# Grid attention tiled by 16 grid columns and 8 rows, in place of two whole grid rows

## The chip, the cores and the metric

The kernel runs on one core of a Trainium2 chip. The metric is the device time of one execution, in microseconds: the median of three was 2283.3 before the change (2283.01 to 2284.41). All times below are microseconds unless marked ns.

## What is computed

Two blocks run one after the other on 512 tokens of width 1024, in float32. The first has two layers of mixed attention and a gated product. The second has two layers: window and latent attention over the tokens and 256 context tokens, and then the grid attention, which is what changes. The 512 tokens are a grid of 8 rows and 64 columns. A query at column c sees, in all 8 rows, the 16 columns from clip(c - 8, 0, 48), with a learned bias by the distance in rows and columns, and beside them all 256 context keys, in one softmax:

```python
rows = s_len // GRID_W                      # 8, GRID_W = 64
kh = min(C_KH, rows)                        # 8
cs = jnp.clip(col - C_KW // 2, 0, GRID_W - C_KW)
col_ok = (col[None, :] >= cs[:, None]) & (col[None, :] < cs[:, None] + C_KW)
...
s_loc = jnp.einsum('bqhd,bkhd->bhqk', qr, kr) * scale + bias
s_loc = jnp.where(mask, s_loc, -jnp.inf)    # mask: col_ok for each of the 8 rows
s_ctx = jnp.einsum('bqhd,blhd->bhql', qr, kc) * scale
p = jax.nn.softmax(jnp.concatenate([s_loc, s_ctx], axis=-1), axis=-1)
return p_loc @ vr + p_ctx @ vc              # 16 heads of 64
...
y = (o * jax.nn.silu(z)) @ out_w
```

## The kernel before, in words

Every engine runs its own program, a list of stages, and stages pass work on by semaphores. Products (line 526) split each factor into a high and a low float32r part and add three matmuls; TensorE takes weights in pieces from two buffers, which ScalarE (`cut_high`, L486) and VectorE (`cut_low`, L491) cut ahead of it.

`WidePairs` (L1712) is the attention of the second block, with `grid=True` for the grid. It walks 8 units, one for each pair of heads, and in each 4 steps, one for each tile of 128 queries, which are two grid rows. Keys of a step are all 512 tokens and 256 context tokens, 768 for each head. Both heads of a step lie in three banks of PSUM, in one of two sets (`base`, L1800), so that TensorE computes the scores of step s+1 before it transposes step s. For each step:
- TensorE, `scores` (L1840): three terms for each head, keys of 512 and 256 columns, in the order `ORDER`. `turn_probs` (L1886): 12 transposes of 128x128. `values` (L1898): 24 matmuls, 6 key tiles for 2 heads, into bank 6. Once a unit `wide` (L1913): 4 transposes of the inverse sums into bank 7.
- VectorE, `grid_iteration` (L2149): `context_max` (L2070), the copy of the first transposed bank (L2116), then for each head an add of the bias with a running maximum (L2086) and its negation (L2088). Once a unit `invert` (L2104, L2109), `pair_low` for the queries and the keys of the next unit (L2211), and `gate_wide` (L2143), inverse sums by silu(z).
- ScalarE: the exponentials (L1971), the copy of the other two transposed banks (L1982), and once a unit `pair_high` (L2206), `copy_o` (L1989), which empties bank 6, and the loads of z and of the bias (L2004, L2007).
- GpSimd: the product of the outputs and the gate (L2193).

The order on ScalarE, in which a step's instructions stand behind each other, is:

```python
for s in range(-1, self.N + 1):
    if 0 <= s < self.N and self.rest[s]:
        copy_probs(s)
    if s + 1 < self.N:
        exps(s + 1)
    ...
    if s - 1 in self.ends:
        copy_o(self.ends[s - 1])
```

The bias: `Start.gpsimd` writes the table of 15x31 values of each head, padded, to a scratch in HBM. `MaskedBias` (L2231), beside the down product of the first layer (`WideProduct.scalar`, L1522), loads shifted windows of it (4 DMAs for a pair of heads, L2247, issued by ScalarE between its cuts), GpSimd adds the column mask (L2259), and the result is stored (L2251). Queries, and the outputs in `Split`, are reversed within a grid row (`backwards`), since the bias is read backwards. `ModNorm` (L2800) is the norm ahead of the second layer: for each of 8 chunks VectorE makes `full` (L2899) and `low` (L2906) with ScalarE's `h_hi` between (L2861), and the product that follows starts while these run. `SiluOut` (L1204) and `CopyOut` (L1113) empty the banks of the products for z and for the queries.

## Time and profile before

| | before |
|---|---|
| median of 3 runs | 2283.3 |
| span of the profiled execution | 2281.6 |
| TensorE busy | 2230.1 (98%) |
| VectorE busy | 1283.6 (56%) |
| ScalarE busy | 925.7 (41%) |
| GpSimd busy | 280.3 (12%) |
| granted TensorE clock, mean | 0.999 |

The span goes from the first to the last instruction of one profiled execution. Its own time is given only as this span; the runs of the table's first row contain in addition what lies around it, 1.7 between the span and the median. A busy share is an average over all stages; the chain of waits says which engine the end waits for. L numbers are lines of the kernel. PE is TensorE, DVE VectorE, ACT ScalarE, POOL GpSimd, PEld the loading of weights, and a name with q the queue of an engine.

### The profile page before, as it was taken

Reading aid. Unit: us, or ns where it says so; the run is one execution under the profiler, and the core shown is the slowest. Engines: PE = TensorE matmul, PEld = TensorE weight load, DVE = VectorE, ACT = ScalarE, POOL = GpSimd, SP = SyncE. Lnnn points to the kernel's source line nnn. Section 1 sums busy time; section 2 is a strip of 40 time slices with the busy share of each in tenths; the row PEclk is TensorE's granted clock in tenths of the full one; section 3 lists DMA queues with packets and bytes.
Section 4 is the critical chain, followed back from the end, with each engine's and each line's share of the span. In section 5 each row is a group of like instructions: output and inputs, shape, how many; then the busy total and the mean of one; then the engine's idle time right before and its main releaser. Section 6 shows DMA issues by size and latency. Waiting matters only on the chain.

```text
span 2281.6 us, 33000 instructions
## 1 busy us (share of the span) xinstructions
PE 2230.1 (98%) x13479; PEld 1852.9 (81%) x13479; DVE 1283.6 (56%) x1884; ACT 925.7 (41%) x1558; POOL 280.3 (12%) x175
## 2 busy tenths in 40 slices
PE   7999999999999999999999999999999999999998
PEld 7876688888888776788888888888888888888887
DVE  4687548964225778459853235414667462225884
ACT  3447743222214347742222223224655342124773
POOL 2001322121332002222111000000100000000000
PEclk9999999999999999999999999999999999999999
DMA  5220025632893210035532421221000214212221
GB/s 161 88 70 2 1 94 181 202 114 75 209 266 89 77 56 1 20 129 185 166 111 75 143 88 48 83 79 42 19 18 16 78 62 164 74 56 75 69 66 56
DMA packets 149417, 205.80 MB, mean 90 GB/s; under 512 B 42485, under 2 KB 95746, under 8 KB 149250
## 3 DMA queue, kind: packets, MB, share of 16 engines
q1 hardware_dynamic: 110288, 169.83, 22.9%
q10 hardware_dynamic: 38914, 33.69, 5.7%
q8 instruction: 107, 1.75, 0.3%
q14 instruction: 44, 0.36, 0.0%
q0 software_dynamic: 64, 0.16, 0.0%
HBM read 188.85 MB, written 14.82 MB: 89 GB/s over the span
## 4 chain that ended last, share of the span: by engine, by line
PE 91%; DVE 4%; ACT 3%; issue 2%; DMA 0%; ACTq 0%; POOLq 0%; DVEq 0%
PE ps L526 68%; PE ps L1858 4%; PE ps L1892 3%; PE ps L2509 3%; PE ps L1909 2%; PE ps L2526 2%; PE ps L2538 2%; DVE probs_t L2116 1%; PE ps L2514 1%; PE ps L733 1%; ACT probs_t L2615 1%; DVE neg_max L2060 1%; PE ps L533 1%; PE ps L2512 1%; PE ps L2546 1%
## 5 line engine op out<-in xcount | busy, mean ns | idle before, releaser
L491 DVE TENSOR_TENSOR w_low<-w_raw,w_high 128x2048 fp32r<-128x2048 f32 (+4 forms) x140 | 303.5, 2168 | 491.6 <-ACT w_high L486 491.4
L486 ACT ACTIVATE w_high<-w_raw 128x2048 fp32r<-128x2048 f32 (+4 forms) x140 | 253.0, 1807 | 602.0 <-PE ps L526 549.9
L526 PE MATMUL ps<-h_hi,w_high 128*128 128x512 f32 (+1 forms) x1168 | 439.6, 376 | 1.2 <-DVE w_low L491 0.6
L526 PE MATMUL ps<-h_lo,w_high 128*128 128x512 f32 (+1 forms) x1168 | 437.3, 374 | 0.0
L526 PE MATMUL ps<-h_hi,w_low 128*128 128x512 f32 (+1 forms) x1168 | 436.9, 374 | 0.0
L526 PEld LDWEIGHTS ps<-h_hi,w_high 128*128 128x128 f32 x1168 | 220.0, 188 | 42.1 <-DVE w_low L491 1.2
L526 PEld LDWEIGHTS ps<-h_hi,w_low 128*128 128x128 f32 x1168 | 219.8, 188 | 39.6
L526 PEld LDWEIGHTS ps<-h_lo,w_high 128*128 128x128 f32 x1168 | 220.0, 188 | 39.3 <-issue 0.5
L526 PE MATMUL ps<-w_high,h_hi 128*128 128x512 f32 (+3 forms) x576 | 214.0, 372 | 0.6 <-DVE h_lo L2906 0.6
L526 PE MATMUL ps<-w_low,h_hi 128*128 128x512 f32 (+3 forms) x576 | 211.6, 367 | 0.0
L526 PE MATMUL ps<-w_high,h_lo 128*128 128x512 f32 (+3 forms) x576 | 211.4, 367 | 0.0
L720 DVE SCALAR_TENSOR_TENSOR ada_acc<-ada_w,cond,ada_acc 128x512 f32<-128x512 f32 x168 | 143.6, 896 | 2.6
L1473 POOL TENSOR_TENSOR gated<-gated,inv_wide 128x512 f32<-128x512 f32 x44 | 96.6, 2215 | 370.4 <-ACT gated L1465 370.4
L526 PE MATMUL ps<-act_hi,w_low 128*128 128x512 f32 x352 | 137.0, 389 | 0.0
L526 PE MATMUL ps<-act_lo,w_high 128*128 128x512 f32 x352 | 137.0, 389 | 0.0
L526 PE MATMUL ps<-act_hi,w_high 128*128 128x512 f32 x352 | 136.9, 389 | 0.0
L1971 ACT ACTIVATE probs<-ps,neg_max 128x768 f32<-128x768 f32 (+3 forms) x160 | 123.4, 783 | 13.8 <-DVE neg_max L2060 9.7
L526 PEld LDWEIGHTS ps<-w_high,h_hi 128*128 128x128 f32 x576 | 108.2, 188 | 22.4 <-issue 7.5
L526 PEld LDWEIGHTS ps<-w_low,h_hi 128*128 128x128 f32 x576 | 108.2, 188 | 16.0
L526 PEld LDWEIGHTS ps<-w_high,h_lo 128*128 128x128 f32 x576 | 108.3, 188 | 15.1
L1468 ACT ACTIVATE act_hi<-gated 128x512 fp32r<-128x512 f32 x44 | 27.6, 633 | 197.1 <-DVE gated L1486 196.4
L2670 DVE TENSOR_REDUCE neg_max<-ps 128x2 f32<-128x256 f32 (+1 forms) x80 | 65.7, 822 | 64.0 <-PE ps L2512 35.4
(372 smaller groups left out, 3869.8 us busy)
## 6 DMA issues: line engine op xcount, KB each, us to landing
w_raw<-in_w_gate_up SPq DMA_DIRECT2D x44, 1024.0 KB, 5.2
ada_w<-in_ada_w SPq DMA_DIRECT2D x24, 1024.0 KB, 5.2
w_raw<-in_w_down SPq DMA_DIRECT2D x20, 1024.0 KB, 5.3
w_raw<-in_w_in SPq DMA_DIRECT2D x16, 1024.0 KB, 5.1
w_raw<-in_c_in_w SPq DMA_DIRECT2D x16, 1024.0 KB, 5.4
w_raw<-in_w_out SPq DMA_DIRECT2D x8, 1024.0 KB, 5.0
w_raw<-in_ab_in_w SPq DMA_DIRECT2D x8, 1024.0 KB, 5.2
mask_table<-bias_scratch ACTq DMA_DIRECT2D x32, 224.0 KB, 7.6
```

Of the source, the lines that this page charges most:

```text
L486: e.activation(w_high[j % 2][:, 0:size], w_raw[j % 2][:, 0:size], ACT.Copy).then_inc(sig.w_high_done, 1)
L491: e.tensor_tensor(w_low[j % 2][:, 0:size], w_raw[j % 2][:, 0:size], w_high[j % 2][:, 0:size].bitcast(F32), ALU.subtract).then_inc(sig.w_lo ...
L526: mm = e.matmul(dst, lhs, rhs, start=start and a == 0, stop=stop and a == 2)
L720: ins = e.scalar_tensor_tensor(out=acc, in0=w, scalar=c, in1=acc, op0=ALU.mult, op1=ALU.add)
L1473: e.tensor_tensor(gated[:, m, :], gated[:, m, :], inv_wide[:], ALU.mult).then_inc(sig.silu_scaled, 1)
L1858: return e.matmul(dst.rearrange("p (b c) -> p b c", c=P), q(m, block), k(m, a, b), start=n == 0, stop=stop and n == 2)
L1892: mm = e.transpose(flat[:, self.base(s) + b * P:self.base(s) + (b + 1) * P], self.probs[s % 2][:, b * P:(b + 1) * P], ident)
L1909: mm = e.matmul(ps[64 * m:64 * m + 64, 6, j * P:(j + 1) * P], x.value(m, self.blocks(s, m)[i]), self.probs_t[s % 2][:, b * P:(b + 1) * P], ...
L1971: ins = e.activation(self.probs[s % 2][:, r * n:(r + 1) * n], self.row(s, r), ACT.Exp, bias=neg_max2[:, c:c + 1], accum_out=sums2[:, c:c + 1])
L2509: e.matmul(ps[:, self.bank(s, m), 0:n], q[x.rows(m), t * P:n], k[x.rows(m), 0:n], start=True, stop=False)
L2526: mm = e.transpose(ps[:, self.bank(s, m), kt * P:(kt + 1) * P], probs1[s % 3][:, m, kt * P:(kt + 1) * P], ident)
L2670: e.tensor_reduce(out=neg_max[:, 2 * s:2 * s + 2], in_=self.both(s, (t + 1) * P), op=ALU.max, axis=AX.X, negate=True).then_inc(sig.max_rea ...
```

## The change

A new stage `GridPairs` takes the place of `WidePairs(grid=True)`. A tile of 128 queries is now 8 grid rows by 16 columns: tile 0 holds columns 0 to 7 and 56 to 63, tiles 1 to 3 the columns 8 to 55 in groups of 16. Keys are laid out in blocks of 16 columns by 8 rows, and each tile sees two of the four blocks (`LOCAL`), so a head has 256 local and 256 context keys, one bank of PSUM. Three sets of two banks hold the scores, which TensorE computes two steps ahead. `add` and one reduction over both heads take the place of the fused add and maximum. `copy_o` and `gate_wide` put the columns back in natural order in two instructions each.

Around it: `ModNorm` writes the 512 tokens of the second layer by blocks of columns, in four instructions a chunk; `QueriesOut` writes queries by tiles, in three instructions for one; z is put back in natural order by the silu; `Split` no longer reverses. The bias is loaded by 8 DMAs for each pair of heads instead of 4, in runs of 32 values instead of 64, masked on GpSimd in four instructions instead of one, and stored and loaded in 512 KB instead of 896 KB. The core of the diff:

```diff
-        probs_t2, probs_t3 = ([at(f"probs_t{n}_{i}", [P, 2 * ALL], F32, base + 24576 + 6144 * i) for i in range(2)] for n, base in ((2, B1 + 19200), (3, R2)))
-        probs2, probs3 = ([at(f"probs{n}_{i}", [P, 2 * ALL], F32, base + 36864 + 6144 * i) for i in range(2)] for n, base in ((2, B1 + 19200), (3, R2)))
+        probs_t2 = [at(f"probs_t2_{i}", [P, 2 * ALL], F32, B1 + 43776 + 6144 * i) for i in range(2)]
+        probs2 = [at(f"probs2_{i}", [P, 2 * ALL], F32, B1 + 56064 + 6144 * i) for i in range(2)]
+        probs_t3 = [at(f"probs_t3_{i}", [P, 2, 512], F32, R2 + 24576 + 4096 * i) for i in range(3)]
+        probs3 = [at(f"probs3_{i}", [P, 2, 512], F32, R2 + 36864 + 4096 * i) for i in range(3)]
...
+        class QueriesOut(CopyOut):
+
+
+            def put(self, e, d, src, mine, m):
+                d = d.rearrange("p (b w v) -> p b w v", w=8, v=16)
+                src = src.rearrange("p (j r x) -> p j r x", r=8, x=16)[:, :, ::-1, :]
+                if mine == 0:
+                    copy = lambda d, s: e.activation(d, s, ACT.Copy, scale=self.scale)
+                else:
+                    copy = lambda d, s: e.tensor_scalar(d, s, self.scale, None, ALU.mult)
+                copy(d[:, 0, :, 8:16], src[:, 3, :, 15:7:-1])
+                copy(d[:, 1:4, :, 8:16], src[:, 0:3, :, 15:7:-1])
+                copy(d[:, :, :, 0:8], src[:, :, :, 7::-1]).then_inc((sig.evac_act, sig.evac_vec)[mine], 1)
...
+        class GridPairs(Stage):
+            U, N = CH // 2, 2 * CH
+            LOCAL = ((0, 3), (0, 1), (1, 2), (2, 3))
+            LOWS_ON_POOL = False
+            def __init__(self):
+                self.cut_at = {4 * p - 6 + c: (p, c) for p in range(1, U) for c in range(2)}
...
+            def head(self, s, m):
+                return ps[:, 2 * (s % 3) + m, :]
+            def both(self, s):
+                return ps[:, 2 * (s % 3):2 * (s % 3) + 2, :]
+            def natural(self, bank):
+                tiles = ps[:, bank, :].rearrange("p (b w v) -> p w b v", w=8, v=16)[:, ::-1]
+                return tiles[:, :, 1:4, ::-1], tiles[:, :, 0, :].rearrange("p r (g x) -> p r g x", g=2)[:, :, :, ::-1]
...
+                def scores(s):
+                    p, b = s // 4, s % 4
+                    if b == 0:
+                        e.wait_ge(sig.qk_ready, B["qk_ready"] + 2 * p)
+                    if s >= 3:
+                        e.wait_ge(sig.turned_ready, B["turned_ready"] + s - 2)
+                        e.wait_ge(sig.turned_second, B["turned_second"] + s - 2)
+                    qs, ks = pair_highs(p)
+                    kl = kc_low[:, p, :].rearrange("p (b c) -> p b c", c=P)
+                    here = slice(b - 1, b + 1) if b else slice(0, 4, 3)
+                    for c, blocks in enumerate((here, slice(4, 6))):
+                        for n in range(3):
+                            for m in range(2):
+                                rows_ = slice(64 * m, 64 * m + 64)
+                                q = qc_low[rows_, p, b * P:b * P + P] if n == 2 else qs[rows_, b, :]
+                                k = (kl if n == 1 else ks)[rows_, blocks, :]
+                                dst = self.head(s, m)[:, c * CTX:(c + 1) * CTX].rearrange("p (b c) -> p b c", c=P)
+                                mm = e.matmul(dst, q, k, start=n == 0, stop=n == 2)
+                    mm.then_inc(sig.scores_ready, 1)
+                def turn_probs(s):
+                    for m in range(2):
+                        e.wait_ge(sig.probs_ready, B["probs_ready"] + 2 * s + m + 1)
+                        for b in range(4):
+                            mm = e.transpose(self.head(s, m)[:, b * P:(b + 1) * P], probs3[s % 3][:, m, b * P:(b + 1) * P], ident)
+                        mm.then_inc(sig.probs_turned, 1)
+
+                def values(s):
+                    u, b = s // 4, s % 4
+                    e.wait_ge(sig.turned_ready, B["turned_ready"] + s + 1)
+                    e.wait_ge(sig.turned_second, B["turned_second"] + s + 1)
+                    if b == 0 and u:
+                        e.wait_ge(sig.o_done, B["o_done"] + u)
+                    for i, kt in enumerate(self.LOCAL[b] + (4, 5)):
+                        for m in range(2):
+                            mm = e.matmul(ps[64 * m:64 * m + 64, 6, b * P:(b + 1) * P], v_c[:, kt, (2 * u + m) * 64:(2 * u + m) * 64 + 64],
+                                          probs_t3[s % 3][:, m, i * P:(i + 1) * P], start=i == 0, stop=i == 3)
+                    mm.then_inc(sig.o_ready, 1)
...
+                scores(0)
+                scores(1)
+                scores(2)
+                keep_warm(e, 6, 6)
+                for s in range(self.N + 1):
+                    if s < self.N:
+                        turn_probs(s)
+                    if s == 1:
+                        keep_warm(e, 6, 3)
+                    if 1 <= s < self.N - 2:
+                        scores(s + 2)
+                    if s % 4 == 3:
+                        wide(s // 4)
+                    if s >= 1:
+                        values(s - 1)
+            def scalar(self, e, B, L, ch):
+                def exps(s):
+                    e.wait_ge(sig.max_ready, B["max_ready"] + s + 1)
+                    for m in range(2):
+                        if s >= 3:
+                            e.wait_ge(sig.probs_turned, B["probs_turned"] + 2 * (s - 3) + m + 1)
+                        c = 2 * s + m
+                        e.activation(probs3[s % 3][:, m, :], self.head(s, m), ACT.Exp, bias=neg_max2[:, c:c + 1],
+                                     accum_out=sums2[:, c:c + 1]).then_inc(sig.probs_ready, 1)
+
+                def copy_second(s):
+                    e.wait_ge(sig.probs_turned, B["probs_turned"] + 2 * s + 2)
+                    if s >= 3:
+                        e.wait_ge(sig.o_ready, B["o_ready"] + s - 2)
+                    e.activation(probs_t3[s % 3][:, 1, :], self.head(s, 1), ACT.Copy).then_inc(sig.turned_second, 1)
+
+                def copy_o(u):
+                    e.wait_ge(sig.o_ready, B["o_ready"] + 4 * u + 4)
+                    if u:
+                        e.wait_ge(sig.o_scaled, B["o_scaled"] + u)
+                    mid, ends = zip(self.cells(o_raw2[:]), self.natural(6))
+                    ch.step(e.activation(ends[0], ends[1], ACT.Copy))
+                    e.activation(mid[0], mid[1], ACT.Copy).then_inc(sig.o_done, 1)
+
+                def load_z(u):
+                    if u:
+                        e.wait_ge(sig.wide_ready, B["wide_ready"] + u)
+                    e.dma_start(z_unit[:], z_dram[:, u, 0:S]).then_inc(sig.z_load0, 16)
+
+                def load_bias(p):
+                    e.dma_start(bias2[p % 2][:], masked_dram[p]).then_inc(sems[f"bias_load{p % 2}"], 16)
+
+                for par in range(2):
+                    e.wait_ge(sems[f"z_store{par}"], B[f"z_store{par}"])
+                load_z(0)
+                load_bias(1)
+                for s in range(-2, self.N + 1):
+                    if s % 4 == 1 and s >= 5:
+                        copy_o(s // 4 - 1)
+                    if 0 <= s < self.N:
+                        copy_second(s)
+                    if s + 2 < self.N:
+                        exps(s + 2)
+                    if s % 4 == 1 and s // 4 + 2 < self.U:
+                        load_bias(s // 4 + 2)
+                    if s in self.cut_at:
+                        p, c = self.cut_at[s]
+                        if p >= 2:
+                            e.wait_ge(sig.scores_ready, B["scores_ready"] + 4 * p - 4)
+                        pair_high(e, p, c)
+                    if s % 4 == 1 and 5 <= s:
+                        load_z(s // 4)
+                copy_o(self.U - 1)
...
+                def maxima(s):
+                    u, b = s // 4, s % 4
+                    e.wait_ge(sig.scores_ready, B["scores_ready"] + s + 1)
+                    if b == 0:
+                        name = f"bias_load{u % 2}"
+                        e.wait_ge(sems[name], B[name] + 16 * (u // 2 + u % 2))
+                    here = self.both(s)[:, :, 0:CTX]
+                    ch.step(e.tensor_tensor(here, here, bias2[u % 2][:, min(b, 1), :, :], ALU.add))
+                    ch.wait(e)
+                    e.tensor_reduce(out=neg_max2[:, 2 * s:2 * s + 2], in_=self.both(s), op=ALU.max, axis=AX.X,
+                                    negate=True).then_inc(sig.max_ready, 1)
+
+                def copy_first(s):
+                    e.wait_ge(sig.probs_turned, B["probs_turned"] + 2 * s + 1)
+                    if s >= 3:
+                        e.wait_ge(sig.o_ready, B["o_ready"] + s - 2)
+                    e.tensor_copy(probs_t3[s % 3][:, 0, :], self.head(s, 0)).then_inc(sig.turned_ready, 1)
...
+                def gate_wide(u):
+                    e.wait_ge(sig.inverse_wide, B["inverse_wide"] + u + 1)
+                    e.wait_ge(sig.z_load0, B["z_load0"] + 16 * (u + 1))
+                    if u:
+                        e.wait_ge(sig.o_scaled, B["o_scaled"] + u)
+                    mid, ends = zip(self.cells(wide2[:]), self.natural(7), self.cells(z_unit[:]))
+                    ch.step(e.tensor_tensor(*ends, ALU.mult))
+                    e.tensor_tensor(*mid, ALU.mult).then_inc(sig.wide_ready, 1)
+
+                for s in range(-2, self.N + 1):
+                    if 0 <= s < self.N:
+                        copy_first(s)
+                    if s % 4 == 0 and s >= 4:
+                        gate_wide(s // 4 - 1)
+                    if s + 2 < self.N:
+                        maxima(s + 2)
+                    if s - 1 in self.cut_at and not self.LOWS_ON_POOL:
+                        p, c = self.cut_at[s - 1]
+                        pair_low(e, B, p, c, 2 * p - 1 + c)
+                    if s % 4 == 2 and s > 0:
+                        invert(s // 4)
+                gate_piece(e, {n: B[n] for n in ("gate_landed", "pair")}, 1, gate_row, 3)
...
             def beside(self, e, B, j):
...
-                    for m in range(2):
-                        for half in range(2):
-                            e.dma_start(mask_tables[n % 4][64 * half:64 * half + 64, m, :, :], bias_source(2 * n + m, half)).then_inc(sems[f"bias_raw{n % 2}"], 16)
+                    for w in range(8):
+                        e.dma_start(bias_raws[n % 4][16 * w:16 * w + 16], bias_source(n, w)).then_inc(sems[f"bias_raw{n % 2}"], 16)
...
+                    e.wait_ge(sems[name], B[name] + 128 * (n // 2 + 1))
+                    for kind, blk, c in self.CUTS:
+                        at_ = CONST_AT["colmask"][0] + 32 * kind + 16 * blk
+                        seen = con[:, at_:at_ + 16].unsqueeze(1).unsqueeze(1).to_broadcast([P, 2, 8, 16])
+                        dst = mask_tables[n % 4][:, kind, :, 128 * blk:128 * blk + 128].rearrange("p m (r x) -> p m r x", x=16)
+                        raw = bias_raws[n % 4][:].rearrange("p (r m) c -> p m r c", m=2)[:, :, :, c:c + 16]
+                        ins = e.tensor_tensor(dst, raw, seen, ALU.add)
+                        if (kind, blk, c) != self.CUTS[-1]:
+                            ch.step(ins)
+                    ins.then_inc(sig.bias_masked, 1)
...
-                        ins = e.scalar_tensor_tensor(out=mod_full[:, k % 2, t0:t0 + nt], in0=src[:, k, :], scalar=self.gain(k, v),
-                                                     in1=ps[:, self.wide_banks[v], 0:nt], op0=ALU.mult, op1=ALU.mult)
+                        dst, x, inv = mod_full[:, k % 2, t0:t0 + nt], src[:, k, :], ps[:, self.wide_banks[v], 0:nt]
+                        if self.l and v == 0:
+                            cuts = [(by_blocks(dst)[:, :, j], by_rows(x)[:, :, j], by_rows(inv)[:, :, j]) for j in range(4)]
+                        else:
+                            cuts = [(dst, x, inv)]
+                        for dst, x, inv in cuts:
+                            ins = e.scalar_tensor_tensor(out=dst, in0=x, scalar=self.gain(k, v), in1=inv, op0=ALU.mult, op1=ALU.mult)
                     ins.then_inc(sig.full_ready, 1)
```

## Rows read from the trace of the kernel before

**Rows 1.** Busy time by engine from first score to next product; (x) instructions, clock, DMA, GB/s.

```profile
2083.60:2232.65 149.05, 146.46 (x1613) 125.63 (x1614) 123.11 (x297) 104.97 (x186) 10.24 (x8) 1.00 0.20 66
```

**Rows 2.** Chain of waits, end of the kernel: start us, us, what.

```profile
2104.11 1.34 PE ps L1858 x9
2105.46 1.46 PE ps L1892 x12
2106.92 0.44 PE ps L1917 x4
2107.35 1.46 PE ps L1909 x24
...
2228.25 0.61 ACT o_raw L1989
...
2232.65 43.80 PE ps L526 x192
```

**Rows 3.** Chain of waits, window attention, one context step.

```profile
1599.10 0.92 PE ps L1858 x12
```

**Rows 4.** Timeline in the grid attention: start us, us, engine, line, what [idle before].

```profile
2119.32 0.68 DVE L2116 COPY probs_t<-ps 128x512 f32<-128x512 f32 x1
2119.92 0.75 DVE L2086 CUSTOM_DVE_ANT_0 ps<-ps,bias,sink_part 128x512 f32<-128x512 f32 x1
...
2120.76 0.16 DVE L2088 TENSOR_SCALAR neg_max<-max 128x1 f32<-128x1 f32 x1
...
2121.09 0.89 ACT L1971 ACTIVATE probs<-ps,neg_max 128x768 f32<-128x768 f32 x1
```

**Rows 5.** Groups by form, grid attention: busy us, mean ns, idle before.

```profile
L1971 ACT ACTIVATE probs<-ps,neg_max 128x768 f32<-128x768 f32 x63 | 56.1, 900 | 1.1 <-DVE neg_max L2088 1.1
L2086 DVE CUSTOM_DVE_ANT_0 ps<-ps,bias,sink_part 128x512 f32<-128x512 f32 x64 | 48.3, 755 | 0.5 <-DVE sink_part L2070 0.2
...
L2116 DVE COPY probs_t<-ps 128x512 f32<-128x512 f32 x31 | 21.1, 681 | 0.2 <-PE ps L1892 0.2
...
L2211 DVE TENSOR_TENSOR kc_low<-k_c,k_high 128x768 fp32r<-128x768 f32 x7 | 6.6, 949 | 0.0
...
L2143 DVE TENSOR_TENSOR wide<-ps,z_unit 128x512 f32<-128x512 f32 x7 | 4.8, 685 | 0.0
L2211 DVE TENSOR_TENSOR qc_low<-q_c,q_high 128x512 fp32r<-128x512 f32 x7 | 4.8, 682 | 0.0
...
L1989 ACT ACTIVATE o_raw<-ps 128x512 f32<-128x512 f32 x7 | 4.1, 590 | 0.0
...
L2109 DVE COPY inv_stage<-sums_inv 128x512 f32<-128x512 f32 x7 | 3.0, 427 | 0.7
...
L2104 DVE RECIPROCAL sums_inv<-sums 128x8 f32<-128x8 f32 x7 | 1.4, 194 | 0.0
```

**Rows 6.** Groups by form, window attention, 1585 to 1800 us.

```profile
L1971 ACT ACTIVATE probs<-ps,neg_max 128x512 f32<-128x512 f32 x16 | 10.9, 687 | 2.1 <-DVE neg_max L2064 2.1
...
L2060 DVE TENSOR_REDUCE neg_max<-ps 128x4 f32<-128x1024 f32 x8 | 9.8, 1223 | 3.0 <-PE ps L1858 2.7
```

**Rows 7.** Line L2899, full of the norms: duration ns min/median/max, first and last start.

```profile
L2899 DVE SCALAR_TENSOR_TENSOR mod_full<-x_t,mod,ps x16: 737/747/749, 1374.9 to 1876.1; 128x512 f32<-128x512 f32 x16
L2899 DVE SCALAR_TENSOR_TENSOR mod_full<-xc_t,mod,ps x16: 473/476/477, 1375.5 to 1876.8; 128x256 f32<-128x256 f32 x16
```

**Rows 8.** Chain of waits from 560 to 720 us.

```profile
559.93 157.76 PE ps L526 x696
```

**Rows 9.** Line L2247, loads of the bias tables.

```profile
L2247 ACTq DMA_DIRECT2D mask_table<-bias_scratch x32: 581/894/5556, 583.2 to 665.9; - x32
```

**Rows 10.** Busy time and granted clock in two short stretches.

```profile
1856.00:1857.00 1.00, 1.00 (x5) 0.99 (x4) 0.49 (x2) 0.00 (x0) 0.00 (x0) 0.50 0.00 0
...
1666.00:1668.00 2.00, 1.41 (x19) 1.17 (x16) 1.28 (x4) 1.99 (x9) 0.00 (x0) 1.00 0.01 4
```

More of the change, by code:

```diff
@@ L1224, in scalar @@
                     done += 1
-                    e.activation(self.buf[:, par, t0:t0 + nt], ps[:, st.bank(i, n), 0:nt], ACT.Silu).then_inc(sig.evac_act, 1)
+                    dst, src = self.to(self.buf[:, par, t0:t0 + nt]), self.view(ps[:, st.bank(i, n), 0:nt])
+                    e.activation(dst, src, ACT.Silu).then_inc(sig.evac_act, 1)
                     if t0 + nt == st.tokens:
@@ L1658, in invert_wide, with __init__ @@
                 self.invert(e, B, inv_wide[:])
-        def backwards(a):
-            return a.rearrange("p (r c) -> p r c", c=64)[:, :, ::-1]
         class Split(Stage):
-            def __init__(self, src, hi, lo, reverse=False, first=0, cut=None):
-                turn = (lambda a: backwards(a)) if reverse else (lambda a: a)
-                self.src = lambda k: turn(src[:, k, :])
-                self.hi, self.lo = ((lambda k, a=a: a[:, k, :].rearrange("p (r c) -> p r c", c=64) if reverse else a[:, k, :]) for a in (hi, lo))
+            def __init__(self, src, hi, lo, first=0, cut=None):
+                self.src, self.hi, self.lo = ((lambda k, a=a: a[:, k, :]) for a in (src, hi, lo))
                 self.first, self.cut = first, cut
@@ L1778, in spread @@
             def spread(self, u):
-                there = not self.grid and u % 2
+                there = u % 2
                 return (wide_there if there else wide2)[:, 0:self.units[u].cols], (z_there if there else z_unit)[:, 0:self.units[u].cols]
@@ L1921, in tensor @@
                     turn(i, i)
-                if not self.grid:
-                    keep_warm(e, 6, 4)
+                keep_warm(e, 6, 4)
                 for s in range(-1, self.N + 1):
@@ L1929, in tensor @@
                     if s == 0:
-                        keep_warm(e, 6, 10 if self.grid else 5)
+                        keep_warm(e, 6, 5)
                     if 0 <= s < self.N:
@@ L1935, in tensor @@
                         turn(i, 7)
-                    if s - 1 in self.ends and (self.grid or s < self.N):
+                    if s - 1 in self.ends and s < self.N:
                         wide(self.ends[s - 1])
@@ L1942, in tensor @@
                         turn(i, 7)
-                if not self.grid:
-                    wide(self.ends[self.N - 1])
+                wide(self.ends[self.N - 1])
             def scalar(self, e, B, L, ch):
@@ L1961, in exps @@
                     n, tiles = self.keys(s), len(self.steps[s][1])
-                    if not self.grid:
-                        e.wait_ge(sig.max_ready, B["max_ready"] + s + 1)
+                    e.wait_ge(sig.max_ready, B["max_ready"] + s + 1)
                     if s >= 2:
@@ L2013, in scalar @@
                 load_z(0)
-                if not self.grid:
-                    load_z(1)
-                if self.grid:
-                    load_bias(1)
+                load_z(1)
                 for s in range(-1, self.N + 1):
@@ L2044, in scalar @@
                         sink_exp(self.ends[s + 1])
-                    if not self.grid and self.N - 6 <= s < self.N - 2:
+                    if self.N - 6 <= s < self.N - 2:
                         high_part(s - self.N + 6)
```

217 lines of the change are left out of this document (92 added, 125 removed).

## The prediction

> **What bounds the kernel now.** I read the page's busy shares first (TensorE 98%, VectorE 56%, ScalarE 41%), then the stretches. The grid attention with its ramps lies between its first score matmul and the first matmul of the product after it: 149.05 us, TensorE busy in 146.46, VectorE in 123.11, ScalarE in 104.97 [rows 1]. The chain of waits inside it is TensorE alone: per step scores 1.34, 12 transposes 1.46, 24 value matmuls 1.46, so 4.26, and once per pair of heads (4 steps) the 0.44 of the wide transposes: 17.48 per pair [rows 2]. The reader is to see that no other engine stands in that chain, but that VectorE and ScalarE have only some 15% and 30% to spare, so they count as soon as TensorE gets shorter. Outside the stretch TensorE runs without a gap except at norms, starts and tails.
>
> **The change, part by part.**
>
> *TensorE.* Write S, T, V, W for the scores, transposes, values of a step and the wide transposes. T falls from 12 to 8: 8/12 of 1.46 = 0.97. V falls from 24 to 16: 0.97. S becomes 12 matmuls of 256 columns, the two heads in turn, which the context steps of the window attention already issue: 0.92 in the chain [rows 3]; with a hand-over 0.93. W stays 0.44. A pair costs 4 x 2.87 + 0.44 = 11.92: the floor, 5.56 below today.
>
> *VectorE.* Instructions overlap by about 0.08: a 0.68 copy is followed after 0.60 [rows 4]. CF (copy of the first bank) stays 0.60. MX (add bias, then one reduction) is an add over 512 elements in PSUM, between the 0.685 of L2143 and the 0.755 of L2086 [rows 5]; I take 0.75, as that writes PSUM too. Then 0.04 and a reduction over 1024, 1.225 [rows 6]: 2.02 to its end, 1.94 until VectorE is free. Removed are the second L2086, its accumulator read and L2088. Per pair come the lows 0.60 and 0.87 (0.682 and 0.949 less overlap), the reciprocal and the staging copy 0.58 (about 0.19 and 0.427), and GW (gate_wide), now two instructions. Its fixed part by 0.682 at 512 and 0.949 at 768 elements is 0.15, so 0.28 and 0.55, less overlap 0.67 [rows 5]. Sum 4 x 2.54 + 0.60 + 0.87 + 0.58 + 0.67 = 12.9.
>
> *ScalarE.* An exp of 512 takes 0.687 [rows 6]; two take EX = 1.42 to the end of the second (their accumulator reads overlap). CS, the copy of the second bank, 0.59. Highs 0.62 and 0.84 and DMA issues 0.9 a pair. CO, the copy of the outputs, was one of 0.590 [rows 5] and is two: exp at 768 against 512 gives 0.21 per 256 elements and 0.26 fixed, so 0.36 + 0.50 = 0.86 (bounds 0.6, if the second costs nothing, and 1.2, at 0.6 each). Sum about 11.4: not the bound by itself.
>
> *The order of the queues.* By sums a pair would take 12.9, but the queues are strict. V of a pair's first step, V(4u+4), needs bank 6 emptied by CO(u). ScalarE issues CO(u) behind EX(4u+6), which waits for MX(4u+6), which stands behind GW on VectorE. Before the change TensorE was long enough to hide this. Now it closes a loop; from the release of V(4u): V 0.97, T 0.97, S(4u+4) 0.93, hop 0.10; MX 1.94, invert 0.58, CF 0.60, MX 1.94, low of the queries 0.60, CF 0.60, GW 0.67, MX to its end 2.02; hop 0.18, EX 1.42, CO 0.86, hop 0.12. Sum **14.50 a pair**, 3.0 less than now. Hops are as the exp that starts 0.17 after VectorE's end [rows 4]. I walked each queue through one pair in this order: VectorE idles for 0.7 before the first of these MX, TensorE for about 1.7 before V(4u+4), and nothing else on the loop arrives later.
>
> *Ramps.* From the first score to MX(4), with the exp table load as now, 12.2: two MX, the low of the queries, MX and low of the keys on VectorE, then CF, MX and S(4). Six loops: 87.0. From MX(28) to the product: 8.35 to the end of MX(30), 2.6 for EX and CO, V, T, V, T, W, V, V = 6.3 with hops, then 4.42 as now from the last value matmul to the product, plus 0.25 for the longer CO [rows 2]: 21.9. Sum 12.2 + 87.0 + 21.9 = 121.1 against 149.05: **27.9 saved**.
>
> *The second norm.* `full` of the 512 tokens becomes four instructions of 128. At 512 and 256 elements it takes 0.747 and 0.476, so 0.205 fixed [rows 7], 0.125 of it not overlapped: +0.38 a chunk, bounds +0.2 and +0.9 (twice the rate for 16-element runs; the reversed rows of L2143 cost nothing extra, so I stay at 0.38). The product behind it starts its second weight piece only after the fifth low, with six such chunks before it, one of them half under ScalarE: **+2.1** (1.0 to 5.0).
>
> *Edits at nothing.* Silu and query evacuations get two more short instructions or strided views, under products in which TensorE is busy all the time; without cover the queries would cost about 0.5 each, 4 in all. The bias tables are cut in the first layer's down product: loads go from 32 with 896 runs of 256 B to 64 with 256 runs of 128 B, GpSimd's add from one of 1792 elements to four of 256, the store from 896 to 512 KB. TensorE is covered by two weight buffers: the chain from 560 to 718 is L526 alone [rows 8]. I take 0; the other end is rival 3. At the start GpSimd issues four DMAs for two, about 1.3 more, before adds that end 9 us before they are read: 0. Split without reversal, the earlier final loads: 0.
>
> **Sum.** 2281.6 - 27.9 + 2.1 = 2255.8 of span. The span lies 1.7 below the median of 2283.3, so **2257.5 us**, 25.8 less (1.1%). Own range 2252 to 2264: half a us on each of seven pairs is 3.5, the norm gives 1 down and 3 up.
>
> **The rivals.**
> 1. *The loop does not bind* (CO and GW run as cheap as their old forms, hops shorter): VectorE's 12.9 a pair. 7 x 1.6 = 11.2 more saved: 2246. For it: the busy sums; against: the order in code. TensorE's floor of 11.92 would give 2239.
> 2. *Short runs cost.* Instructions over runs of 8 or 16 elements (CO, GW, the norm) at double rate: 1.5 a pair, 3 at the norm: 2271. L2143 with its reversed rows speaks against it.
> 3. *The bias loads hold ScalarE (slower).* Place: the down product at 583 to 680 us. An issue of these loads takes 581 to 5556 ns, median 894 [rows 9], because the queue is full. A piece lasts 48 matmuls, 10.9. ScalarE needs cut 1.9, store issue 1.2, waits about 4, and 8 issues where there were 4. At 0.894 each it runs 3.4 over per piece, 24 in seven, less some 5 of cover (a piece of 10.9 less its two cuts, 4.3, partly used already): 2276. The whole is slower from about 1.0 us an issue; at 1.6 each, 9 over per piece, it is 57 more, 2315. Against it: the runs fall from 28672 to 16384 and the bytes from 7.3 to 2.1 MB, so the queue should be emptier, not fuller.
> 4. *The clock falls (slower).* TensorE's granted clock is 1.00 in the whole stage now. It was 0.50, the 1.2 GHz level, at 1856 to 1857, just after a wait of 0.8 and matmuls of one column [rows 10]. In the changed stage TensorE waits 1.7 in each pair. At 1.2 GHz throughout, TensorE's 11.92 would be 23.8 a pair, 8 x 6.3 more than now less some 4 at the ramps: about 2332; slower from the point where half of the stage runs at that level (11.92 x 1.47 = 17.5). Against it: 1666 to 1668, with TensorE idle for 0.6 of 2.0 between dense work, at 1.00 [rows 10]. The Trainium skill (TensorE: Matmul & The Clock Gate, part 4 on transposes) says that transposes do not keep the clock up as matmuls do. By that rule a third of the changed stage would count as rest on top of the wait; the present stage is a third transposes as well, 1.46 of 4.26, at 1.00, and so disagrees.
>
> **How the numbers follow.** Forecast (2252 to 2264) 58%, rival 1 with its floor 20%, rival 2 and other sizes between 2264 and 2279 12%, rival 3 beyond that 5%, rival 4 4%, 1% near no change. Range for 8 in 10: 2243 to 2271, which takes in rival 1 and most of rival 2. A difference of 0.2%, 4.6 us, is about what a measurement can tell. Faster 0.91, same 0.02, slower 0.07.
>
> **What would show it.** Between first score and product about 121 us. In the chain per pair S near 0.93, T and V near 0.97, and a wait of TensorE of 1 to 2 us before one V in four, released by o_raw on ScalarE; if that wait is missing and VectorE is busy throughout, it was rival 1. Clock at 1.00. The norm's chain near 1858 to 1874 longer by 2. L526 alone in the chain between 580 and 680; anything else there is rival 3. CO or GW beyond 1.2 together with a period over 15 is rival 2. The forecast is wrong if the period lies outside 13.8 to 15.3, or another stage moves by more than 3 us.

## The result, and the profile after

The changed kernel takes **2255.11 us** (median of 4 runs, 2254.17 to 2255.68) against 2283.26 for the kernel before on the same chip (2283.01 to 2284.41): ratio 0.9874, interval 0.986 to 0.9888, 28.2 us less. The forecast was 2257.5 (own range 2252 to 2264). The profiled execution has a span of 2253.9, 27.7 less than before.

First the stretch from the first score matmul of the grid attention to the first matmul of the product after it (busy time of each engine, granted clock last but two), against [rows 1]:

```profile
2085.89:2204.90 119.01, 106.84 (x1226) 89.10 (x1226) 102.52 (x145) 78.02 (x194) 10.27 (x8) 0.99 0.18 59
```

The stage is 30.0 shorter and starts 2.3 later: that is the whole difference of 27.7. TensorE, which left only 2.6 of 149.05 unused before, now leaves 12.2 of 119.01. The chain of waits shows where. One pair of heads, in answer to [rows 2]:

```profile
2124.37 1.09 PE ps L2245 x16
2125.47 1.02 PE ps L2234 x8
2126.49 0.91 PE ps L2227 x12
...
2130.35 0.59 PE ps L2254 x4
2130.94 1.02 PE ps L2245 x16
2131.96 1.04 PE ps L2234 x8
...
2133.02 0.68 DVE probs_t L2344
2133.70 0.20 DVE wide L2362
2133.90 0.47 DVE wide L2363
2134.36 0.62 DVE ps L2335
...
2135.00 1.23 DVE neg_max L2337
...
2136.85 0.86 ACT probs L2280 x3
2137.71 0.17 ACT o_raw L2294
2137.88 0.39 ACT o_raw L2295
...
2138.40 1.09 PE ps L2245 x16
```

L2245 are the values (V), L2234 the transposes (T), L2227 the scores (S), L2254 the wide transposes (W). The pair lasts 14.03, and its end is the copy of a bank, GW, MX, the exps and CO, in the order in which the prediction's loop had them.

In the middle this chain stays on TensorE only because the transposes end at 2133.00, just before the copy of the bank starts at 2133.02. That copy (`copy_first`) waits only for the first head's half of them, which ends 0.60 into the piece, near 2132.56. What it stood behind is VectorE's own queue, which from the end of the first scores on has no gap above 0.1:

```profile
2127.44 0.70 DVE L2335 TENSOR_TENSOR ps<-ps,bias 128x512 f32<-128x512 f32 x1 [0.66 <-PE ps L2227]
2128.17 1.23 DVE L2337 TENSOR_REDUCE neg_max<-ps 128x2 f32<-128x1024 f32 x1
2129.32 0.19 DVE L2349 RECIPROCAL sums_inv<-sums 128x8 f32<-128x8 f32 x1
2129.61 0.43 DVE L2354 COPY inv_stage<-sums_inv 128x512 f32<-128x512 f32 x1
2129.95 0.68 DVE L2344 COPY probs_t<-ps 128x512 f32<-128x512 f32 x1
2130.55 0.69 DVE L2335 TENSOR_TENSOR ps<-ps,bias 128x512 f32<-128x512 f32 x1
2131.28 1.23 DVE L2337 TENSOR_REDUCE neg_max<-ps 128x2 f32<-128x1024 f32 x1
2132.42 0.68 DVE L2156 TENSOR_TENSOR qc_low<-q_c,q_high 128x512 fp32r<-128x512 f32 x1
2133.02 0.68 DVE L2344 COPY probs_t<-ps 128x512 f32<-128x512 f32 x1
```

So the loop is V, T, S on TensorE (3.03), then VectorE, which has waited 0.66 for them and then works with no gap above 0.1 up to the last reduction, then ScalarE.

Four pairs in a row last 14.03 (2124.37 to 2180.48), the one after them 13.70. TensorE's waits, at the first two of them (idle time in brackets):

```profile
2108.78 1.79 PE L2245 MATMUL ps<-probs_t,v_c 128*64 128x128 f32 x16 [1.74 <-ACT o_raw L2295]
2124.37 1.09 PE L2245 MATMUL ps<-probs_t,v_c 128*64 128x128 f32 x16 [1.56 <-ACT o_raw L2295]
```

The same 16 matmuls take 1.79 in the first row and 1.09 in the second. The granted clock around the first:

```profile
2107.00:2109.00 2.00, 0.26 (x6) 0.25 (x6) 1.97 (x4) 2.00 (x7) 0.23 (x1) 1.00 0.00 0
2109.00:2110.00 1.00, 1.00 (x14) 1.00 (x12) 0.94 (x1) 0.15 (x2) 1.00 (x1) 0.51 0.00 0
2110.00:2112.00 2.00, 2.00 (x13) 1.67 (x10) 0.35 (x1) 1.42 (x4) 0.04 (x1) 0.50 0.53 80
2112.00:2114.00 2.00, 2.00 (x27) 1.54 (x27) 0.93 (x2) 0.60 (x1) 0.00 (x0) 0.89 0.83 322
```

It was at 0.50, the 1.2 GHz level, from 2109.0 to 2112.4, and this one pair lasts 15.59 (2108.78 to 2124.37) instead of 14.03: 1.56 lost. In every other stretch of the stage the clock is at 1.00.

The forms behind the terms between 2100 and 2196 us (mean ns of one), in answer to [rows 5, 6]:

```profile
L2280 ACT ACTIVATE probs<-ps,neg_max 128x512 f32<-128x512 f32 x56 | 38.0, 683 | 30.9 <-DVE neg_max L2337 30.9
L2337 DVE TENSOR_REDUCE neg_max<-ps 128x2 f32<-128x1024 f32 x27 | 33.1, 1225 | 0.9
L2335 DVE TENSOR_TENSOR ps<-ps,bias 128x512 f32<-128x512 f32 x27 | 18.7, 693 | 4.7 <-PE ps L2227 4.7
L2156 DVE TENSOR_TENSOR kc_low<-k_c,k_high 128x768 fp32r<-128x768 f32 x6 | 5.7, 948 | 0.0
```

Two chains outside the stage: the second norm, whose full part is now five instructions a chunk, 1.51 to 1.52 where it alone stands in the chain; and the down product in which the bias tables are cut, in answer to [rows 8].

```profile
1858.26 1.52 DVE mod_full L3077 x5
...
1873.85 2.21 DVE w_low L495
1876.06 0.04 issue
1876.11 2.12 PE ps L530 x8
```

```profile
559.99 157.99 PE ps L530 x697
```

### The profile page after: what moved, and what is told of

The parts are those of the page before. It is cut to its first block, busy times and chain, and to the rows that moved or that the text cites. A ratio compares the mean times of both kernels' runs of the same rounds, so it can differ in the third digit from the quotient of the medians.

```text
span 2253.9 us, 32118 instructions
## 1 busy us (share of the span) xinstructions
PE 2191.1 (97%) x13091; PEld 1816.6 (81%) x13091; DVE 1266.2 (56%) x1764; ACT 899.4 (40%) x1574; POOL 266.5 (12%) x201
## 4 chain that ended last, share of the span: by engine, by line
PE 88%; DVE 5%; ACT 3%; issue 3%; ACTq 0%; DMA 0%; POOLq 0%; DVEq 0%
PE ps L530 69%; PE ps L2681 3%; PE ps L1873 3%; PE ps L2698 2%; PE ps L2710 2%; PE ps L2245 1%; DVE probs_t L2088 1%; PE ps L2234 1%; PE ps L2686 1%; PE ps L737 1%; PE ps L1907 1%; ACT probs_t L2787 1%; DVE neg_max L2055 1%; DVE neg_max L2337 1%; PE ps L537 1%
## 5 line engine op out<-in xcount | busy, mean ns | idle before, releaser
L530 PEld LDWEIGHTS ps<-w_high,h_lo 128*128 128x128 f32 x576 | 108.3, 188 | 15.1
L2775 ACT ACTIVATE probs<-ps,neg_max 128x128 f32<-128x128 f32 (+3 forms) x160 | 82.8, 526 | 9.9 <-DVE neg_max L2842 9.6
```

Source lines behind the costliest of these rows:

```text
L530: mm = e.matmul(dst, lhs, rhs, start=start and a == 0, stop=stop and a == 2)
L2775: ins = e.activation(probs1[s % 3][:, m, 0:n], ps[:, self.bank(s, m), 0:n], ACT.Exp, bias=neg_max[:, c:c + 1], accum_out=sums[:, c:c + 1])
```

## The experiments

All times are medians of four or more runs on the same chip as runs of the kernel before; "the pair" is the distance from one GpSimd product of outputs to the next in the profiled execution, which repeats to 0.02 where the clock stays up (0.1 in e3), and "stage" is the stretch from the first score to the next product. The changed kernel was not timed again beside the experiments; the kernel before was, at 2283.57 to 2283.71 against the 2283.26 beside the changed kernel, so differences to the changed kernel carry some 0.5 of that, and e9 ran on another chip. Most kernels also have single runs 2 to 4 us above their lowest, so a median of four can shift by 1 or 2 us; the pair and the stage are the finer measure.

| kernel | us | ratio to before, interval | pair | stage |
|---|---|---|---|---|
| changed kernel | 2255.11 | 0.9874 (0.986 to 0.9888) | 14.03, one 15.59 | 119.0 |
| e1 copy early | 2250.56 | 0.9858 (0.9843 to 0.9873) | 13.52 | 113.7 |
| e2 lows on GpSimd | 2252.12 | 0.9862 (0.9849 to 0.9876) | 13.70 | 115.2 |
| e3 both | 2244.93 | 0.9829 (0.9815 to 0.9842) | 12.41 | 106.6 |
| e4 one step ahead | 2289.30 | 1.0023 (1.0013 to 1.0032) | 17.72, two 18.37 | 152.2 |
| e5 norm in one | 2251.61 | 0.9858 (0.9841 to 0.9874) | 14.03 | 117.5 |
| e6 copy in seven | 2259.97 | 0.9895 (0.988 to 0.991) | 14.33, two of 15.70 and 15.51 | 122.6 |
| e7 early, product later | 2244.87 | 0.9831 (0.9816 to 0.9846) | 12.62 | 108.3 |
| e8 whole copies | 2253.42 | 0.9869 (0.9854 to 0.9883) | 13.90 | 116.6 |
| e9 copy in thirteen | 2266.87 | 0.9925 (0.9912 to 0.9939) | 14.69, three of 16.06 to 16.25 | 127.0 |

**e1: the copy of the outputs early.**

```
-                    if s % 4 == 1 and s >= 5:
-                        copy_o(s // 4 - 1)
                     if 0 <= s < self.N:
                         copy_second(s)
+                    if s % 4 == 0 and s >= 4 and s < self.N:
+                        copy_o(s // 4 - 1)
```

> The copy of a pair's outputs (CO) is issued before the exps of step 4u+6 and no longer behind them. Theory (the loop): what holds a pair at 14.03 us is V(4u+4) waiting for this copy behind those exps; once the copy no longer hangs on the maxima, the loop is open, TensorE's wait of 1.55 to 1.7 a pair goes, and the period falls to the larger of TensorE's own work (4 x (1.02 + 1.02 + 0.91) + 0.59 = 12.4) and VectorE's (4 x 2.49 + 2.7 = 12.6). Over seven pairs 1.4 to 1.6 each: 10 to 11 us less than the changed kernel, 2244 to 2246. Rival (VectorE sets the period already and TensorE's wait only shows it): at most 2 us less. Second rival (ScalarE's queue: its exps come later behind a copy that waits for V(4u+3)): a new wait before T in step 4u+6, and between 0 and 5 us less.

Measured: 4.6 less than the changed kernel, not 10. The wait of V(4u+4) is gone, so the loop was there; but the pair fell only to 13.52, and VectorE is busy in 49.11 of 50 us (2112 to 2162). The timeline shows what it does with them (second column the duration):

```profile
2119.49 1.28 POOL L2390 TENSOR_TENSOR o_all<-o_raw,wide 128x512 f32<-128x512 f32 x1 [12.24 <-ACT o_raw L2295]
2119.74 1.84 DVE L2156 TENSOR_TENSOR kc_low<-k_c,k_high 128x768 fp32r<-128x768 f32 x1
```

The low of the keys takes 1.84 in each of six pairs and 0.948 in the changed kernel. With the copy early, GpSimd's product starts 0.25 before it. The expectation's second rival asked for a new wait before T in step 4u+6. There is a new wait of TensorE, 0.63 a pair, but it stands before T in step 4u+7, and the exps it waits for start only after ScalarE itself has waited 2.29 for VectorE's maxima behind that long low: it is VectorE's lateness, not ScalarE's queue. e7 tests this.

**e2: the two lows of a pair on GpSimd.**

```
-            LOWS_ON_POOL = False
+            LOWS_ON_POOL = True
```

> The two subtractions a pair that cut queries and keys (0.60 and 0.87 on VectorE) go to GpSimd, nothing else. Theory (the loop): VectorE's share falls to some 11.1 a pair, but the middle of the loop runs through TensorE and the last stretch through GW, MX, exps and CO, none of which is shortened: within 2 us of the changed kernel. Rival (VectorE sets the period): 1.47 a pair, about 10 us less, 2245. A loss of up to 3 us if GpSimd's subtractions slow VectorE down or hold up its product of a pair's outputs.

Measured: 3.0 less, a little over the bound given for the loop, far from rival 1's 10. The pair is 13.70: of the 0.60 for the low of the queries, 0.33 came off the pair. In the changed kernel VectorE comes to the copy of the bank straight from that low, 0.46 after the first half of T. In e2 the low is gone and the copy starts right behind the first half of T, 0.60 into it:

```profile
2115.91 0.60 PE ps L2234 x4
2116.54 0.06 DVE probs_t L2344
...
2117.14 0.28 DVE wide L2362
```

So the low did stand in the loop, as the prediction had it, and with the low gone TensorE's way to the same point (V, T, S, V, T, S, W, V and half of T) takes over, 0.43 shorter; 0.10 of that is lost again between the copy and the reduction. The expectation for this run had the middle of the loop on TensorE, with nothing in it to shorten; that was its error. Of the 3.8 by which the stage is shorter, about 1.6 is the fall of the clock that this execution did not have.

**e3: both.** The diff is that of e1 and of e2.

> Both edits: the copy of the outputs early, and the subtractions on GpSimd. Theory (the loop): with the loop open and VectorE at 11.1 a pair only TensorE's own work of 12.4 is left: 2243 to 2245, at most 2 less than the early copy alone. Rival (VectorE sets the period): the same as the subtractions on GpSimd alone.

Measured: 10.2 less than the changed kernel, the time foreseen, but not for the reason foreseen, since e1 alone had not got there. The four runs fall into two groups, 2242.86 and 2243.22, 2246.64 and 2246.88, and the median lies between them. Over four pairs of the profiled execution (one of the lower group) TensorE is busy without a gap, 12.41 a pair, which is its own work:

```profile
2106.57:2156.28 49.71, 49.71 (x598) 41.48 (x596) 45.14 (x65) 38.36 (x98) 17.39 (x14) 1.00 0.20 65
```

**e4: the tiles kept, one step ahead instead of two.** The core of it:

```
-                    if 1 <= s < self.N - 2:
-                        scores(s + 2)
+        (scores(s + 1) stands before turn_probs(s))
-                        exps(s + 2)
+                        exps(s + 1)
-                        maxima(s + 2)
+                        maxima(s + 1)
```

> The small tiles kept, but scores, maxima and exps run one step ahead of the transposes and not two (the bias load moves one step later with them). By the changed kernel's rows the chain of one step would then be: hop 0.18, first exp 0.69, half of the transposes with a hop 0.65, copy of the first bank 0.68, add and reduction 1.87, so 4.1 a step, 16.4 a pair, and GW 0.67 on top where it comes in between: about 17.1 against 14.03, 21 us more than the changed kernel over seven pairs, near 2276 to 2279. That would mean that the smaller tiles alone bring only some 5 of the 28 us. Rival (the work of the engines decides, not the order): a step is bounded by VectorE's 12.6 a pair, and the time stays within 5 us of the changed kernel.

Measured: 2289.3, 34 more than the changed kernel and 5.7 more than the kernel before. The direction is the theory's, the size was underestimated: of the 33.2 by which the stage is longer, six pairs take 22.2 (17.72 each and not 17.1, two of them 18.37), the ramp at the start 4.7 and the one at the end 6.2, and the expectation had counted neither ramp. The granted clock fell to 0.50 four times in the stage, once in each ramp and once in each of the two longer pairs. One step in the chain:

```profile
2122.42 0.68 DVE probs_t L2344
2123.11 0.62 DVE ps L2335
2123.75 1.24 DVE neg_max L2337
...
2125.59 0.20 ACT probs L2280
2125.84 0.67 PE ps L2234 x4
```

Each engine works while the others wait. The smaller tiles without the second step ahead bring nothing: TensorE has 5 us less to do per pair and waits for longer than that.

**e5: the second norm in one instruction.**

```
-  cuts = [(by_blocks(dst)[:, :, j], by_rows(x)[:, :, j], by_rows(inv)[:, :, j]) for j in range(4)]
+  cuts = [(dst, x, inv)]
```

> The second norm multiplies its 512 tokens in one instruction and not in four of 128; left out is the reordering of those tokens from rows to blocks. Theory: the four cost 0.38 us a chunk on the chain of this norm, so the first matmul after it comes 2.0 earlier and the time is 2.0 less than the changed kernel, 2253.1. Rival (the path from the norm goes through the high parts on ScalarE, which the four instructions do not lengthen): within 0.5.

Measured: 3.5 less. The chain of the norm gives the 2.0 (first product matmul at 1874.08 against 1876.11):

```profile
1865.15 1.14 DVE mod_full L3077 x2
```

The rest lies in the grid: the first score is 2.2 earlier, and the stage is 117.5 against 119.0 with the same pair of 14.03, because in this execution the clock did not fall.

**e6: the copy of the outputs in seven instructions**, in its old place.

```
-                    e.activation(mid[0], mid[1], ACT.Copy).then_inc(sig.o_done, 1)
+                    for w in range(3):
+                        for r in (slice(0, 4), slice(4, 8)):
+                            last = e.activation(mid[0][:, r, w], mid[1][:, r, w], ACT.Copy)
+                    last.then_inc(sig.o_done, 1)
```

> The copy of the outputs (CO) in its old place behind the exps, but its second instruction of 384 elements cut into six of 64. By the 0.15 between the starts of the two of now, and fixed parts up to 0.2, CO goes from 0.82 to 1.4 to 1.9. Theory (the loop): the excess stands in the loop once a pair, 0.6 to 1.1 by six or seven pairs, 4 to 7 us more than the changed kernel, 2259 to 2262. Rival (VectorE sets the period): ScalarE has over 2 us a pair to spare, within 1 us.

Measured: 4.9 more. The release of V comes 1.10 after CO's start and no longer 0.79, 0.31 later, and the pair is 14.33, 0.30 longer: what CO costs, the pair costs. ScalarE, busy in some two thirds of the stage, is on the path all the same. The five more instructions were cheaper than expected (0.06 each); two of the six distances are longer still, where the clock fell: 15.70, and 15.51 for the last, which is 0.33 shorter than the others where the clock stays up (13.70 in the changed kernel).

**e7: the copy early, and GpSimd's product behind VectorE's low of the keys.** Added to e1:

```
                     e.wait_ge(sig.o_done, B["o_done"] + u + 1)
+                    if u + 2 < self.U:
+                        e.wait_ge(sig.qk_ready, B["qk_ready"] + 2 * (u + 2))
```

> The early copy of the outputs, and GpSimd's product of a pair now waits for VectorE's low of the keys too, so that the two no longer run at once. With the early copy alone that low took 1.85 us where it takes 0.95 in the changed kernel, and in its trace GpSimd's product of 1.28 began 0.25 before the low did each time. Theory (two engines on operands in SBUF hold each other up): the low is 0.95 again, the pair falls from 13.50 to VectorE's 12.6, 5 to 6 us less than the early copy alone, 2244 to 2246. Rival (the low is long for a reason of its own, as the high of the keys written just before): no change, 2250.

Measured: 5.7 less than e1, 2244.87. The same two instructions, one after the other:

```profile
2119.06 0.95 DVE L2156 TENSOR_TENSOR kc_low<-k_c,k_high 128x768 fp32r<-128x768 f32 x1
2120.18 1.28 POOL L2392 TENSOR_TENSOR o_all<-o_raw,wide 128x512 f32<-128x512 f32 x1 [11.34 <-DVE kc_low L2156]
```

The pair is 12.62, VectorE's own sum of 12.6 from the rows of the changed kernel. The low is 0.89 shorter and the pair 0.90: the low's lengthening is what e1 lacked. One added wait is worth nearly as much as moving both lows to another engine (stage 108.3 against 106.6 in e3).

**e8: CO and GW as one instruction each.**

```
-                    ch.step(e.activation(ends[0], ends[1], ACT.Copy))
-                    e.activation(mid[0], mid[1], ACT.Copy).then_inc(sig.o_done, 1)
+                    e.activation(o_raw2[:], ps[:, 6, :], ACT.Copy).then_inc(sig.o_done, 1)
-                    ch.step(e.tensor_tensor(*ends, ALU.mult))
-                    e.tensor_tensor(*mid, ALU.mult).then_inc(sig.wide_ready, 1)
+                    e.tensor_tensor(wide2[:], ps[:, 7, :], z_unit[:], ALU.mult).then_inc(sig.wide_ready, 1)
```

> CO and GW as one instruction each over 512 elements in a row instead of 128 + 384 in runs of 8 or 16; left out is the reordering of the columns from blocks to rows. By the 0.68 and 0.59 of such forms against 0.75 and 0.64 for the pairs of now, the theory (the loop, which holds both) gives 0.15 to 0.3 a pair, 1 to 2 us less than the changed kernel, 2253.1 to 2254.1. Had the short runs cost as the second rival of the prediction said, it would be 1.5 a pair, 10 us.

Measured: 1.7 less, the pair 13.90, 0.13 shorter. The profiled execution had no fall of the clock (stage 116.6), so of the median's 1.7 only 0.13 x 7 = 0.9 is sure to be the loop's.

**e9: the copy in thirteen.** As e6, with four slices of two rows for the two of four.

> As the copy in seven, but with twelve instructions of 32 elements behind the first, to make TensorE's wait before V(4u+4) longer still. By the copy in seven (the release 0.31 later, and the pair 14.33 instead of 14.03) six more instructions make it 0.4 to 0.8 later still. What is open is the clock: it fell once in the changed kernel, behind a wait of 1.74, and twice inside the stage with the copy in seven, whose waits are 1.69 to 2.04, and each fall made its pair 1.2 to 1.6 longer. If a longer wait is what brings it down, it falls in most of the seven pairs here: 0.7 to 1.1 for the loop and 1.2 to 1.6 for the clock by seven, 13 to 19 us more than the changed kernel, 2268 to 2274. If the falls have nothing to do with the length of the wait: one or two of them, 5 to 10 more, 2260 to 2265.

Measured: 11.8 more, between the two cases, of which the stage accounts for 8.0 (127.0 against 119.0). In the profiled execution the first score was already 3.3 late, in a part that the edit does not touch: the clock had fallen there too, from 267.6 to 274.5 us, and the product matmul that starts at 282.74 in the changed kernel starts at 286.81.

```profile
268.00:274.00 6.00, 6.00 (x30) 4.67 (x28) 0.90 (x3) 2.70 (x7) 0.52 (x1) 0.50 0.00 0
```

TensorE's longest wait in the 14 us before that fall was 0.37, and the changed kernel has the same wait in the same place and kept its clock.

The steady pair is 14.69, 0.36 for six instructions. TensorE's waits in this kernel, of which the second and third ended in pairs of 16.25 and 16.06 with the clock down, the first and fourth did not:

```profile
2112.70 1.09 PE L2245 MATMUL ps<-probs_t,v_c 128*64 128x128 f32 x16 [2.40 <-ACT o_raw L2297]
2127.39 1.53 PE L2245 MATMUL ps<-probs_t,v_c 128*64 128x128 f32 x16 [2.21 <-ACT o_raw L2297]
2143.64 1.09 PE L2245 MATMUL ps<-probs_t,v_c 128*64 128x128 f32 x16 [2.22 <-ACT o_raw L2297]
2159.70 1.09 PE L2245 MATMUL ps<-probs_t,v_c 128*64 128x128 f32 x16 [2.07 <-ACT o_raw L2297]
```

In the stage, longer waits go with more falls: none or one at waits of 1.22 to 1.74 (one in the changed kernel, none in e2, e5 and e8), two at 1.52 to 2.04 (e6), three at 1.88 to 2.40 (e9), each from one profiled execution. The length alone does not say which pair it will be: in e9 the falls came behind 2.21, 2.22 and 2.21 and not behind 2.40. Why it falls behind one wait and not behind the next of equal length stays open, and so does the fall at 268 with no such wait before it.

## Why the prediction was right

The prediction's mechanism and its time hold. Its loop was 0.47 a pair too long, 2.8 us over six pairs, and about half of that was hidden by a fall of the clock (1.5) that it had not priced. That part of the agreement is luck, though without the fall the time would be some 2253.6 and still in its own range. The stage measured 119.0 against 121.1, the first score came 2.3 and not 2.1 later, and the median lies 0.6 below the profiled execution; together these make up the 2.4 between 2257.5 and 2255.1.

- **The loop: right.** Its end is the chain of the profile, e6 shows that the pair lengthens by what CO lengthens, and e1 shows that TensorE's wait goes when CO no longer stands behind the exps. By pieces, predicted and measured: V, T, S 2.87 and 3.03; from S to GW 6.36 and 6.22; GW 0.67 and 0.66; MX to its end 2.02 and 1.94; exps with the hop before them 1.60 and 1.49; CO with its hop 0.98 and 0.69; sum 14.50 and 14.03. The overestimates are the add in each MX (0.75 taken, 0.693 measured), the hops into MX and the exps (0.10 and 0.18 taken, 0.04 each measured) and CO (0.86 taken from two full instructions; the second starts 0.16 after the first).
- **The route through the middle: right.** The prediction led it through VectorE (MX, invert, CF, MX, low, CF), and VectorE's rows run in that order with no gap above 0.1. The chain of waits shows TensorE there (V, T, S, W, V, T), but its T is not what the copy of the bank waited for; e2, which takes the low out, shortens the pair by 0.33 and so shows that the low stood in the loop, and that TensorE's route is close behind. The waits come out too: 0.66 on VectorE before the first MX (0.7 predicted) and 1.55 on TensorE (about 1.7).
- **TensorE's floor: too low.** V and T take 1.02 and not 8/12 and 16/24 of their old times (0.97), and W 0.59 against 0.44. The floor of 11.92 is 12.41 in e3.
- **VectorE's sum** of 12.9 is 12.6 in e7: the add again.
- **Ramps: right.** 34.1 predicted, 33.4 measured. From the first score to the start of MX(4) it took 12.0 (12.2 predicted), with the four MX and two lows of the prediction's list. From the start of MX(28) to the product it took 21.35 and not 21.9: 8.46 to the end of MX(30) (8.35), 2.17 for the exps and CO (2.6), 6.5 for V, T, V, T, W, V, V (6.3) and 4.2 to the product (4.67). The six loops between took 85.65, the one with the clock down among them, instead of 87.0.
- **The norm: right**, +2.1 predicted; the product behind it starts 2.03 earlier in e5. The first score is 2.3 later than before, so the edits taken at nothing that lie ahead of it cost about 0.2 together.
- **Rival 1 (the loop does not bind)** did not come, but its number is what e7 gives once the loop is opened: 2246 predicted for VectorE as the bound, 2244.9 measured. The rival's other bound, TensorE's floor at 2239, is 2244.9 in e3 (its lower two runs 2243.0), since the floor was too low.
- **Rival 2 (short runs cost)** falls with e8: 0.13 a pair where it asked for 1.5.
- **Rival 3 (the bias loads)**: the chain from 560 to 718 is TensorE alone. The 64 loads take a median of 0.47 to issue, where the 32 larger ones took 0.89 [rows 9], and the mean busy share of the 16 DMA engines was 0.60 from 580 to 590 us and 0.78 from 590 to 600, where it had been 0.90 and 1.17: fewer bytes and a queue less full, as argued against it.
- **Rival 4 (the clock)** is not refuted, it came in small. The prediction priced only a clock that stays down for half the stage or more; there was one fall of 3.4 us for 1.56, and e5, whose waits sum to the same 10.7 us, had none. The Trainium skill's remark that transposes do not keep the clock up (TensorE: Matmul & The Clock Gate, part 4) is not borne out where transposes alternate with matmuls: e3 runs TensorE without a gap with over a third of its time in transposes (4.67 of 12.41), at 1.00 throughout the stage. No run here has transposes alone.

Where the gain comes from: TensorE's work falls by 5.1 a pair (17.48 to 12.41), and 3.45 of them arrive. e4 shows that the second step ahead is what lets them arrive; without it the change is slower than the kernel before. The 1.6 that don't arrive stand in TensorE's wait for the copy of the outputs, and e3 gets all of them back and e7 1.4: both beat the changed kernel by 10.2 in the median, and the kernel before by 38.7 and 38.8.

## What to carry to other kernels

When an edit shortens the engine that was busy all the time, walk the strict queues of the others through one period before adding up busy shares: an instruction of 0.8 us on an engine one third idle set the period here, by what it was queued behind. Open such a loop by moving the releasing instruction ahead of whatever waits for a later step, and then look at what newly runs side by side. A chain of waits names the engine whose work ended last before a start, and where two end within 0.02 of each other that can be the wrong one: look in the code for what the instruction waits for, and in its engine's own rows for what it stood behind. Here the smaller tiles needed more steps in flight: without the second step ahead this change was a loss.

## What the hardware did that was not expected

- **GpSimd's product held VectorE up.** VectorE's subtraction of 768 elements, both inputs in SBUF, took 1.84 instead of 0.95 beside GpSimd's product of 1.28, which itself stayed at 1.28 (e1), ending 0.81 after that product did, and 0.95 again when the product came after it (e7). Instructions of VectorE with an input in PSUM were not lengthened: beside GpSimd's lows in e3, copy, add and reduction keep 0.68, 0.70 and 1.23. The Trainium skill (GPSIMD Engine Reference, section 1, Specifications) says that GpSimd shares its interfaces to SBUF with VectorE and contends with instructions that have two inputs there; e1 and e7 agree.
- **The clock fell behind some waits of 1.7 to 2.2 us in otherwise dense work**, each time for about 3.4 us at a price of 1.4 to 1.6, and not behind others as long (the changed kernel, e6, e9). Once, in e9 at 268 us, it fell with no wait above 0.37 before it, for 6.9 us.
- **A copy on ScalarE cut finer costs little:** 0.06 for each further instruction of 64 or 32 elements (e6, e9). In the changed kernel the second of the two starts 0.16 after the first, which lasts 0.27.
